# The block sums of a fast matrix product: made on TensorE by accumulated turns and one difference per pair of tiles

## The reference, cut to what matters

```
def swiglu(x, w1, w3, w2):
    return (jax.nn.silu(x @ w1) * (x @ w3)) @ w2
def half_ffn(x, i, n):
    h = 0.5 * swiglu(x, ffn_w1[i, n], ffn_w3[i, n], ffn_w2[i, n])
    return layer_norm(ALPHA * x + h, ln_g[i, 2 * n], ln_b[i, 2 * n])
...
x = layer_norm(ALPHA * x + m, ln_g[i, 1], ln_b[i, 1])
x = half_ffn(x, i, 1)
gate = jax.nn.sigmoid(x @ ple_w_gate[i] + ple_b_gate[i])
e = p_i @ ple_w_proj[i]
return layer_norm(ALPHA * x + gate * e, ln_g[i, 3], ln_b[i, 3])
```

## Time and profile before

| | |
|---|---|
| median of 3 runs | 2495.22 us (2495.19 to 2495.64) |
| the profiled execution | 2500.3 us |
| its span, first to last instruction | 2498.6 us |
| TensorE busy (matmuls) | 2427.4 us, 97% |
| VectorE busy | 1660.6 us, 66% |
| ScalarE busy | 1102.9 us, 44% |
| GpSimd busy | 470.5 us, 19% |
| mean granted TensorE clock | 0.990 |

### The profile page before, as it was taken

One profiled execution on the slowest core, in us unless ns is written; L12 is line 12 of the kernel. 1 busy time (PEld: TensorE's weight loads), 2 busy tenths in 40 slices (PEclk: granted clock), 3 DMA queues, 4 the chain that ended last, 5 costly groups with the idle time before them and its releaser, 6 DMA issues.

```text
span 2498.6 us, 38673 instructions
## 1 busy us (share of the span) xinstructions
PE 2427.4 (97%) x15358; PEld 2174.5 (87%) x15358; DVE 1660.6 (66%) x2166; ACT 1102.9 (44%) x1769; POOL 470.5 (19%) x399
## 2 busy tenths in 40 slices
PE   7999999989999999899999999999999999999998
PEld 7999999879999998799999988777776799999986
DVE  5866666877666676776666662666666776666667
ACT  4433343344333343543344333666665443344343
POOL 4211123222211110311121101122123321111100
PEclk9999999999999999999999999999999999999999
DMA  4322222223222223132222225777876132322231
GB/s 132 94 79 85 85 85 93 60 73 98 75 85 85 85 94 94 41 95 85 85 85 85 84 77 148 207 194 206 230 203 182 45 109 80 95 85 73 82 102 68
DMA packets 376642, 259.14 MB, mean 104 GB/s; under 512 B 10321, under 2 KB 339025, under 8 KB 376464
## 3 DMA queue, kind: packets, MB, share of 16 engines
q1 hardware_dynamic: 371360, 239.64, 33.3%
q0 software_dynamic: 5104, 17.04, 2.1%
HBM read 248.22 MB, written 8.42 MB: 103 GB/s over the span
## 4 chain that ended last, share of the span: by engine, by line
PE 86%; DVE 7%; ACT 3%; issue 3%; DMA 1%; POOL 0%; SPq 0%; DVEq 0%; ACTq 0%
PE ps L2496 77%; PE ps L797 5%; PE ps L829 2%; DVE ring L1884 1%; DVE x L1956 1%; DVE x L1942 1%; DVE small L1902 1%; PE ps L905 0%; ACT ring L1373 0%; DMA raw<-in_ffn_w_dram 0%; PE ps L2545 0%; PE ps L2602 0%; ACT e_buf L1582 0%; ACT xt_hi L1391 0%; POOL t_buf L1151 0%
## 5 line engine op out<-in xcount | busy, mean ns | idle before, releaser
L2496 PE MATMUL ps<-xt_hi,ring 128*128 128x320 f32 (+2 forms) x3328 | 791.2, 313 | 22.3 <-DVE tmp L2052 8.7
L2496 PEld LDWEIGHTS ps<-xt_hi,ring 128*128 128x128 f32 x3328 | 576.7, 191 | 35.1 <-DVE tmp L2052 9.6
L2496 PE MATMUL ps<-ring,h_hi 128*128 128x512 f32 x1760 | 556.7, 392 | 8.5 <-DVE x L1942 4.6
L1884 DVE TENSOR_TENSOR ring<-raw,ring 128x1024 fp32r<-128x1024 f32 (+1 forms) x318 | 437.2, 1378 | 129.3 <-ACT ring L1373 129.1
L2496 PE MATMUL ps<-xt_lo,ring 128*128 128x320 f32 (+2 forms) x1664 | 518.8, 312 | 0.0
L2496 PE MATMUL ps<-s_ops,ring 128*128 128x320 f32 x3168 | 510.5, 311 | 7.7 <-DVE s_ops L2015 7.7
L2496 PEld LDWEIGHTS ps<-s_ops,ring 128*128 128x128 f32 x3168 | 479.5, 189 | 8.7 <-DVE s_ops L2015 8.7
L2496 PEld LDWEIGHTS ps<-ring,h_hi 128*128 128x128 f32 x1760 | 331.5, 188 | 82.8 <-DVE x L1942 6.3
L1373 ACT ACTIVATE ring<-raw 128x1024 fp32r<-128x1024 f32 (+1 forms) x318 | 287.3, 931 | 238.0 <-PE ps L2496 211.8
L1151 POOL TENSOR_TENSOR t_buf<-raw,t_buf 128x512 f32<-128x512 f32 x88 | 115.9, 1317 | 1346.0 <-DVE t_buf L1897 1346.0
L2496 PE MATMUL ps<-ring,h_lo 128*128 128x512 f32 x880 | 344.0, 391 | 0.0
(11 more groups left out here) (188 smaller groups left out, 2505.4 us busy)
## 6 DMA issues: line engine op xcount, KB each, us to landing
raw<-in_ffn_w_dram SPq DMA_DIRECT2D x264, 512.0 KB, 4.1
k_raw<-in_cache_k_dram SPq DMA_DIRECT2D x128, 256.0 KB, 5.0
v_raw<-in_cache_v_dram SPq DMA_DIRECT2D x128, 256.0 KB, 4.3
raw<-in_sb_w_in_dram SPq DMA_DIRECT2D x24, 512.0 KB, 5.5
raw<-in_ple_w_gate_dram SPq DMA_DIRECT2D x16, 512.0 KB, 3.9
g_b<-in_ln_g_dram POOLq DMA_DIRECT2D x8, 512.0 KB, 5.6
b_b<-in_ln_b_dram POOLq DMA_DIRECT2D x8, 512.0 KB, 7.1
raw<-in_sb_w_out_dram SPq DMA_DIRECT2D x8, 512.0 KB, 5.8
```

The source lines that it names most:

```text
L1884: ve.tensor_tensor(ring[:, slot, 1, col:col + cols], conversion_source(u), ring[:, slot, 0, col:col + cols].bitcast(F32), ALU.subtract).th ...
L2496: return pe.matmul(out, w, xx, start=first, stop=last, skip_group_check=True)
```

## The change

The four stage changes into a feed-forward stage (from load, pool, embed of layer 0, and out) are altered in the same way.

- S1 to S4 of a pair are no longer made in token order. `turn_sums12` turns both halves of tile 2 or 3 into one bank, accumulating, which gives S1; it does so again in the next bank and subtracts the high and the low part of x11 there with `neg_ident`, which gives S2. `turn_sums43` turns one half of the pair's difference for S3 and accumulates both halves for S4.
- The difference of a pair is one VectorE instruction of 1,024 columns (`left_diffs` and `right_diffs`). GpSimd's `pair_sums` is gone.
- The banks of S12b and S43a are swapped, and the orders on TensorE, ScalarE and VectorE are new, with `gate_of_first` of chunk 0 and `first_product` of chunk 0 put into the stage before, item C0 behind B0, and `first_diffs` of chunk 1 behind `low_sums43` of pair b.
- In embed, VectorE makes the low parts of x0, x1, x2; turns and subtractions move by some matmuls in out and embed. In v and embed the first subtraction for the stage before moves from the third to the fifth group of matmuls.
- In pool, `spread(2)` and `normalise(2)` stand ahead of `first_diffs` of the next stage and of `mix(3)`.

```diff
-BLOCK_PIECES = (("x0", 4), ("x1", 6), ("x2", 4), ("S12a", 6), ("S12b", 4), ("S43a", 6), ("S43b", 6), ("X22", 6))
+BLOCK_PIECES = (("x0", 4), ("x1", 6), ("x2", 4), ("S12a", 6), ("S43a", 4), ("S12b", 6), ("S43b", 6), ("X22", 6))
...
-            by_act = st.kind != "load" and name[0] == "x"
+            by_act = st.kind in ("ffn", "pool", "out") and name[0] == "x"
...
             gate(1)
-            if st.prev.kind != "load":
+            if st.prev.kind == "load":
+                up(0)
+                first_diffs(0)
                 gate(2)
-            up(0)
-            first_diffs(0)
-            if st.prev.kind == "load":
+            else:
                 gate(2)
+                first_diffs(0)
+                up(0)
...
# ScalarE, start of a feed-forward stage
+                if prev.kind == "load":
+                    first_product(st, 0)
+                    cvt_to(unit["B", 0] + 1)
+                    first_product(st, 1)
+                    silu_of_first(st, 0)
+                    hi_sums12(prev, 0)
+                    hi_sums43(prev, 0)
+                    hi_sums12(prev, 1)
+                    cvt_to(unit["A", 2] + 1)
+                else:
                     se.preload_act_table(ACT.Silu)
-                first_product(st, 0)
-                cvt_to(unit["B", 0] + 1)
-                first_product(st, 1)
-                silu_of_first(st, 0)
-                hi_sums12(prev, 0)
-                hi_sums12(prev, 1)
-                cvt_to(unit["A", 2] + 1)
-                hi_sums43(prev, 0)
+                    hi_sums12(prev, 0)
+                    first_product(st, 1)
+                    hi_sums43(prev, 0)
+                    hi_sums12(prev, 1)
+                    cvt_to(unit["C", 0] + 1)
+                    silu_of_first(st, 0)
                 first_product(st, 2)
                 silu_of_first(st, 1)
                 cvt_to(unit["D", 0] + 1)
...
# VectorE, the pair differences, and the start of a feed-forward stage
+                ve.tensor_tensor(pair_diff[:, 0, :], x[:, 0, :], x[:, 2, :], ALU.subtract).then_inc(diff_a, 1)
...
+                ve.tensor_tensor(pair_diff[:, 1, :], x[:, 1, :], x[:, 3, :], ALU.subtract).then_inc(diff_b, 1)
...
                 if prev.kind == "load":
-                    pair_sums12(prev)
-                    pair_sums43(prev)
+                    left_diffs(prev)
+                    right_diffs(prev)
                     gate_of_first(st, 0)
+                    low_sums12(prev, 0)
+                    cvt_to(unit["B", 0] + 1)
+                    low_sums43(prev, 0)
+                    gate_of_first(st, 1)
+                    low_sums12(prev, 1)
+                    cvt_to(unit["A", 2] + 1)
                 else:
-                    gate_of_first(st, 0)
-                    pair_sums12(prev)
-                low_sums12(prev, 0)
-                cvt_to(unit["B", 0] + 1)
-                low_sums12(prev, 1)
-                gate_of_first(st, 1)
-                cvt_to(unit["A", 2] + 1)
-                if prev.kind != "load":
-                    pair_sums43(prev)
-                low_sums43(prev, 0)
+                    cvt_to(unit["B", 0] + 1)
+                    low_sums12(prev, 0)
+                    gate_of_first(st, 1)
+                    cvt_to(unit["C", 0] + 1)
+                    low_sums43(prev, 0)
+                    low_sums12(prev, 1)
+                    right_diffs(prev)
                 cvt_to(unit["D", 0] + 1)
+                low_sums43(prev, 1)
                 first_diffs(st, 1)
-                low_sums43(prev, 1)
+                hidden_of_first(st, 0)
                 cvt_to(unit["B", 1] + 1)
-                hidden_of_first(st, 0)
                 up_of_second(st, 0)
                 cvt_to(unit["D", 1] + 1)
                 low_x22(prev)
...
# VectorE, pool
                     mix(2)
                     low(prev, 4)
+                    spread(2)
+                    normalise(st, 2)
                     first_diffs(st.next, 0)
                     mix(3)
                     low(st, 0)
-                    spread(2)
-                    normalise(st, 2)
                     low(st, 1)
...
                     normalise(st, 3)
+                    left_diffs(st)
                     spread(4)
-                    normalise(st, 4)
+                    centre(st, 4)
+                    gate_of_first(st.next, 0)
+                    rescale(st, 4)
...
# VectorE, embed
                         evacuate(st, TILES + t)
+                        if t in (2, 3):
+                            low(st, t - 2)
                         if t < 3:
                             centre(st, t)
                             add_bias(TILES + t + 1)
                             rescale(st, t)
-                        if t in (2, 3):
-                            low(st, t - 2)
                         if t == 3:
                             add_bias(TILES + t + 1)
+                            low(st, 2)
                             centre(st, t)
...
# TensorE
+            def turn_sum(bank, first, second):
+
+                for block in (first, second):
+                    for c in range(HC if block is not None else 0):
+                        ins = turned(ps[:, bank, c * P:(c + 1) * P], block[:, c * P:(c + 1) * P], block is first and c == 0)
+                return ins
...
+                turn_sum(bank, x[:, 2 + b, 0:HK], x[:, 2 + b, HK:])
+                turn_sum(bank + 1, x[:, 2 + b, 0:HK], x[:, 2 + b, HK:])
+                for xx in (xt_hi, xt_lo):
+                    ins = mm(ps[:, bank + 1, :].rearrange("p (c t) -> p c t", t=P), neg_ident[:],
+                             xx[:, 0:HC, pair_columns(b)], False, True)
...
+                turn_sum(bank, pair_diff[:, b, 0:HK], None)
+                turn_sum(bank + 1, pair_diff[:, b, 0:HK], pair_diff[:, b, HK:]).then_inc(piece_full, 1)
...
                     turn_sums12(prev, 0)
+                    turn_sums43(prev, 0)
                     product2(st, 1)
                     turn_sums12(prev, 1)
-                    turn_sums43(prev, 0)
                     if prev.kind == "load":
                         product1(st, 2)
-                    else:
-                        product2(st, 2)
+                    product2(st, 2)
                     product5(st, 0)
+                    turn_sums43(prev, 1)
                     product6(st, 0)
-                    turn_sums43(prev, 1)
-                    if prev.kind == "load":
-                        product2(st, 2)
                     product3(st, 0)
```

More of the change, by code:

```diff
@@ L369, in streaming_trunk @@
         sums3 = place("work", "sums3", [P, HK], start=t_at - 4 * HK)
-        sums_right = place("work", "sums_right", [P, 4, HK], start=h_at + 8 * D_MODEL)
+        pair_diff = place("work", "pair_diff", [P, 2, D_MODEL], start=h_at + 8 * D_MODEL)
         band = place("work", "band", [P, len(WINDOWS), 3, P], start=t_at)
@@ L1264, in _ @@
                     quarter_of(st)
-                    pair_sums(st)
                 if st.kind == "ffn":
@@ L1807, in _ @@
                             hi(st, t - 2)
+                        if t == 3:
+                            hi(st, 2)
+                        if t == 4 and st.then == "blocks":
+                            first_product(st.next, 0)
                         deviation(st, t)
-                        if t in (2, 3):
-                            low(st, t - 2)
                         if t < TILES - 1:
@@ L2382, in _ @@
                         evacuate(st, TILES + j)
-                        normalise(st, j)
-                        if 1 <= j <= 3:
-                            low(st, j - 1)
+                        if j == TILES - 1:
+                            centre(st, j)
+                            gate_of_first(st.next, 0)
+                            rescale(st, j)
+                        else:
+                            normalise(st, j)
                         if j == 2:
@@ L2428, in _ @@
                             rescale(st, t)
-                        if t in (2, 3):
-                            low(st, t - 2)
                         if t == 3:
                             add_bias(TILES + t + 1)
+                            low(st, 2)
                             centre(st, t)
+                    if st.then == "blocks":
+                        cvt_to(st.next.item["A", 2] + 1)
                     rescale(st, TILES - 2)
                     if st.then == "blocks":
-                        cvt_to(st.next.item["A", 2] + 1)
-                    normalise(st, TILES - 1)
+                        left_diffs(st)
+                        centre(st, TILES - 1)
+                        gate_of_first(st.next, 0)
+                        rescale(st, TILES - 1)
+                    else:
+                        normalise(st, TILES - 1)
                 if st.kind == "pool":
@@ L2696, in product5 @@
                     pe.wait_ge(*lowered(st.prev.piece["S12b"][0]))
```

(1 more changed line is left out.)

96 lines of the change are left out of this document (32 added, 64 removed).

## The result

| | before | after |
|---|---|---|
| median of the timed executions | 2495.43 us (2495.19 to 2499.37, 4) | 2519.18 us (2517.83 to 2521.12, 4) |
| the profiled execution, its span | 2500.3, 2498.6 | 2518.68, 2517.0 |

The ratio is 1.0092, 95% interval 1.0075 to 1.0109: slower by 0.9%, or 23.75 us by the medians. The two spans differ by 18.4 us.

A forecast was written before the change was run, and what follows sets the result against it. TensorE's matmuls bound it, busy in 97% of the span, with time lost in waits at four stage changes. Out +3.9, embed -1.6, pool +8.8, load +5.9 sum to +17.0 us: 2517.3, less the median's 5.1, 2512.2; range 2501 to 2520.

The forecast's parts named there:

- Ahead of product 5 of chunk 0: Feed-forward stages after pool, embed and out: a new wait of 3.0 us for VectorE's low part of S12b.
- From L to product 5 of chunk 2: From S43b's low part done (L): late raw buffer and weight DMA make this stretch 17.95 us, where the trace had 15.86.
- From E to L: From the end of product 1 of chunk 2 (E) to S43b's low part done (L): 19.15 us with clock fall.
- Embed, -1.6: Stage change from embed: front 4.85 us earlier, stretch 44.15 plus 0.7 for a clock fall against 41.65; net -1.6 us.
- Load, +5.9: Stage change from load: L at 45.5, then 17.95 more, ending at 63.45 us where it was 57.57; +5.9 us.
- Pool, +8.8: Stage change from pool: product 1 7.0 us later, 2.4 of half clock, stretch 44.15 against 44.83; +8.8 us.
- Out +3.9: Stage change from out: stretch 44.15 us against 39.88, less a saved wait of 0.4; +3.9 us.
- the last one: Whole kernel: from the profiled execution's 2517.3 us to the runs' median, taken as 5.1 lower, 2512.2.
- The raw buffer doesn't bind: Rival, up weights of chunk 2: DMA lands in 3.9 us or first_diffs come early enough; 9.8 less, 2502; chance 0.12.
- The pool front doesn't move: Rival, pool stage: ScalarE's deviation comes before the mixes; 7.0 and 2.4 us less, 2503; chance 0.10.
- The turns themselves lower the clock: Rival, all four stages: up to 28 successive turns cost one more clock fall each; +7 us, 2519; chance 0.13.
- The faster rival: Moved first_diffs in five places cost nothing, GpSimd and DMA still in time; 9.4 and 9.8 less, 2493.0; chance 0.10.

The follow-up runs named there:

- Runs 1: Changed kernel with first_diffs of chunk 0 in the pool stage put back ahead of spread(2) and normalise of tile 2: 2509.24 us.
- run 2: Changed kernel with first_diffs of chunk 1 put back ahead of the low half of S43b in all four feed-forward stages: 2504.37 us.
- run 3: Changed kernel with ScalarE's rounding of C of chunk 0 (in load, A of chunk 2) ahead of its roundings of S12b: 2507.05 us.
- e6_before_pool: Kernel before with only the pool order changed, first_diffs of chunk 0 behind tile 2's statistics and rescaling: 2506.63 us against 2497.57.
- run 7: Kernel before with first_diffs of chunk 1 behind the low half of S43b, and hidden_of_first ahead of the conversion of B1: 2510.13 us.
- Run 5: Changed kernel with the edits of runs 1, 2 and 3 and two VectorE orders: load's A2 before low S12b, elsewhere low S12a before B0; 2478.7 us, ratio 0.9924.
- run 11: The changed kernel measured once more, unaltered, beside more executions of the kernel before: 2520.8 us, ratio 1.0091.
- run 8: Changed kernel with GpSimd's loads of the two gain rows issued behind its differences of chunk 2 instead of chunk 1: 2508.74 us.

## Why the prediction came out as it did

The forecast was 2512.2 with 2501 to 2520, the measurement 2519.18: the direction and the places were right, the size 7 us short, at the edge of the range. Point by point:

- **The waits, right.** Ahead of product 5 of chunk 0: forecast 3.0, 2.99 in three stages. From L to product 5 of chunk 2: forecast 17.95; 18.13, 17.81 and 17.80 (18.33 in load). Pool's product 1: forecast 7.0 later, it is 12.51 later than the earlier trace rows, 5.19 of it from upstream, 7.3 its own. Runs 1, 2, 3 and 6 show the waits in the three later stages and in pool by taking one away or putting it in alone, run 7 with one more move beside it. Inside the second stretch the parts fell otherwise: ahead of product 3 of chunk 1 TensorE waited 1.34 to 1.87 us, not 2.3, and ahead of product 5 of chunk 2 it waited 0.90.
- **From E to L, 0.5 short.** Forecast 19.15, 19.63 in pool and 19.66 in out: 12 matmuls ran at half clock and the part of a fall was 1.55, not 1.3.
- **Embed, -1.6 forecast, -0.2 measured.** Product 1 came 4.6 earlier, as reckoned (4.85). Between E and S12b's turns there is a wait of 1.17 that I hadn't foreseen: the early product 1 brings forward TensorE's need for S12a, while VectorE still has `rescale` of tile 2 (2.13 us beside GpSimd's rounding, 1.28 elsewhere), the difference of pair a, centring, gating and `rescale` of tile 3 and the conversion of B0 ahead of it. Run 5 took it away by moving that conversion behind the low half of S12a. The start had no half clock, where I had put 0.7.
- **Load, +5.9 forecast, +6.45 measured.** Product 1 began 0.82 later than before. That isn't the change: the same instructions brought it at 14.90 in run 11 and between 14.9 and 15.7 over these runs. So the stage's own loss is 5.6, and L at 45.69 hit the forecast 45.5 in part by luck: counted from product 1 it came 0.6 sooner than reckoned, and the stretch behind it was 0.4 longer (18.33). Why A of chunk 2 is late in load I had half wrong: ScalarE's order is harmless there (run 3), VectorE's is not (run 5).
- **Pool, +8.8 forecast, +9.4 measured** (14.56 - 6.45, and the 1.3 that came back in between); the terms as written add up to 8.7. The three products at its start lost 2.1 to the half clock, forecast 2.4. Out +3.9 forecast, +4.0 measured.
- **The step that failed was the last one**, "The runs' median lies 5.1 below it, 2495.22, and becomes 2512.2". The four stages lost 2.7 us more than the forecast +17.0 (embed 1.4, pool and load 0.6 each, out 0.1), and 1.3 came back outside them by the clock, so the sum missed the 18.4 of the spans by 1.4; the shift of 5.1 was the larger error. I had carried the distance between one execution and three timed ones over to another kernel. Before took 2493.6 to 2501.4 us over its executions beside the experiments, with a profiled one of 2500.3 near the top; the changed kernel's profiled executions, 2518.68 and 2520.06, lie at its medians. With no shift the forecast would have been 2517.3. Said the other way round: a sum drawn from one execution near the top of the old kernel's band gave 17.0, where the medians differ by 21.2 to 23.75. The range held this error by its width; no term of the sum foresaw it.
- **The rivals.** "The raw buffer doesn't bind": false, and its price of 9.8 was too small: run 2 makes it 14.8, since 15.86 was no length at full clock. "The pool front doesn't move": false by its own row. "The turns themselves lower the clock": false. From E on, 16 turns, two subtractions with neg_ident, 12 turns, a product, another 16 turns, two more subtractions and a product follow each other without a break (windows of the changed kernel, behind out and at product 5 of chunk 0):

```profile
1995.59:2005.00 9.41, 9.41 (x74) 8.92 (x71) 3.38 (x6) 4.06 (x8) 0.00 (x0) 1.00 0.01 2
2007.99:2011.34 3.35, 3.35 (x13) 3.31 (x13) 2.21 (x2) 0.00 (x0) 0.00 (x0) 0.51 0.23 69
```

  Full clock through 44 turns, half behind the wait of 2.99. The time of that rival, 2519, was hit all the same, by other terms; a right number is no witness for a mechanism. The Trainium skill (TensorE: Matmul & The Clock Gate, Part 4: PE-mode transpose) says that transposes don't count as activity as matmuls do. The kernel asks for that mode in every turn (`is_transpose=True`), and the trace shows no sign of it: a granted clock of 1.00 over 44 turns with 28 matmuls among and behind them. No run has a longer stretch of turns alone.
- **The faster rival**, "the moved weight differences cost nothing": false, but it named the two places that cost most, and as edits they paid: runs 1 and 2 by themselves 24.7 us.

What stays open: the medians differ by 21.2 to 23.75 us, the profiles by 18.4 to 19.7. I hold that it is where short half-clock stretches happen to fall; no run separates this from other causes. What the turned sums themselves are worth stays open too: e5_two_more, 19 us below the kernel before, has them together with the hoisted gating, embed's low parts on VectorE and the new orders, and no run takes one of these out.

## What to carry to other kernels

Count what stands behind a waiting instruction in its engine's queue, not only what it waits for: the costs here were instructions with ready inputs behind one that was idle, and five changes of order alone (e5_two_more) turned +0.9% into -0.8%. When a length is taken over from a trace as "the rest", read the granted clock in it first, or a clock fall that the change removes is counted twice. And one profiled execution's distance to the median belongs to that execution, not to the kernel.

## What the runs showed of the hardware

- **One kernel's half-clock stretches move.** The same 44 instructions of TensorE behind the same wait of 2.91 us, in the profiled execution of the kernel before:

```profile
443.98:453.20 9.22, 9.22 (x44) 8.07 (x45) 7.96 (x11) 1.24 (x2) 3.61 (x8) 0.66 0.52 123
```

  and in that of e6_before_pool, which is the same program up to there:

```profile
443.44:449.79 6.35, 6.35 (x44) 5.85 (x45) 5.16 (x7) 1.24 (x2) 3.61 (x8) 1.00 0.41 77
```

  In the changed kernel, behind 2.92 us:

```profile
450.45:458.38 7.93, 7.93 (x44) 6.97 (x45) 6.70 (x9) 1.24 (x2) 3.59 (x8) 0.78 0.42 90
```

  2.9 us between the first two, in a kernel whose executions differ by 8. The third is 1.3 shorter than the first: that is what came back between load and pool.
- **An accumulating fp32 turn costs what a plain one does**: 16 in 1.91 us (half of them accumulate) and 12 in 1.47 (a third) with their tails, against 8 in 1.03, all 0.10 from start to start.
- **A 512 KB weight load beside GpSimd's two gain loads** takes 6.4 us, without them 3.9 (run 8).
- **VectorE beside GpSimd**: `rescale` of one tile takes 2.13 us while GpSimd rounds the quarter sums, 1.28 alone (embed, changed kernel):

```profile
1044.41 2.99 POOL L1165 TENSOR_TENSOR s_ops<-sums,s_ops 128x256 fp32r<-128x256 f32 x2
...
1046.35 2.13 DVE L1949 SCALAR_TENSOR_TENSOR x<-x,small,b_b 128x1024 f32<-128x1024 f32 x1
...
1051.44 1.28 DVE L1949 SCALAR_TENSOR_TENSOR x<-x,small,b_b 128x1024 f32<-128x1024 f32 x1
```

  The Trainium skill (SBUF — State Buffer, Who interferes with whom) says that a VectorE instruction with two inputs in SBUF contends with a GpSimd instruction that reads SBUF. The rows agree, with 0.85 us; no run moved GpSimd's work away from it.
